# The way into head 0: a third late down chunk, half a token chunk ahead of the heads, and decay gates by token

## The chip, the cores and the metric

One NeuronCore of a Trainium2 chip runs the whole program; the other seven do nothing. The metric is the device time of one execution in microseconds (us). An execution is made of instructions on five engines that run side by side and wait for each other through semaphores: TensorE (PE, matrix products and transposes; its weight loads are shown as PEld), VectorE (DVE), ScalarE (ACT), GpSimd (POOL) and SyncE (SP, which only issues DMAs here).

## What is computed

Two transformer-like blocks over one sequence of 256 tokens with 1024 channels, all in float32. The change lies where the first feed-forward of the second block ends and its mixer begins:

```python
h = h + 0.5 * swiglu(rmsnorm(h, ffn1_norm[l]), ffn1_w_in[l], ffn1_w_out[l])
h = h + hybrid_mixer(rmsnorm(h, mix_norm[l]), w_in[l], ...)

def hybrid_mixer(u, w_in, ...):
    proj = (u @ w_in).astype(f32)
    (hq, hf, hi, hg, gq, gk, gv, ga, gb, gz, gate_h, gate_g) = jnp.split(proj, offsets, axis=-1)
    ...
    qkv = jax.nn.silu(causal_short_conv(jnp.concatenate([gq, gk, gv], axis=-1), conv_w))
    ...
    beta = jax.nn.sigmoid(gb)
    g = -jnp.exp(a_log.astype(f32)) * jax.nn.softplus(ga + dt_bias)
```

`ga` and `gb` are 16 columns each: the decay gates, 32 columns of `w_in` for all heads together. Every other part of `proj` is wide and is cut by head. `g` goes through a cumulative sum over chunks of tokens and then multiplies the scores of every head.

## The kernel before

**Numbers.** Every weight chunk (128 x 2048 values, 1 MB) comes from memory into a ring of three slots `w_raw`. ScalarE rounds it into `w_hi` (line 623, or in two halves line 630), VectorE takes the rest into `w_lo` (line 1160), and TensorE makes three products per tile: high by high, high by low, low by high, in the one-pass format fp32r. The activations are split the same way into `xa_hi` and `xa_lo`. In all, each chunk costs ScalarE one copy, VectorE one subtraction, and TensorE 48 products with 256 moving columns or 24 with 512.

**The ring sets the order.** Chunks have a global number. The copy into `w_hi` of chunk c waits until TensorE has done chunk c-3 (`gemm_done`), and the load of c waits for the `w_lo` of c-3 (`lo_ready`). Each engine's program is written out by hand in its own order, and an engine takes its instructions strictly in that order.

**The end of the feed-forward** (`ffn`, `last_rows`). Hidden tiles come two to a step: `up` chunks make them, ScalarE and VectorE turn them into `xb`, and a `down` chunk adds their part of the result into PSUM. The last step runs up, up, down, up, up, and then two down chunks together in `last_rows`: tokens 0 to 127 of both (semaphore `y_first`), then tokens 128 to 255 (`y_half`, `gemm_done`). Behind each VectorE adds the residual (line 1403), ScalarE makes the norm's factor and VectorE applies it (line 1517).

**The seam** (`normed`, `first_gemm`, lines 2090 to 2099). TensorE transposes tokens 0 to 127 (line 2083, 8 transposes), runs 2 filler products (`spin`, line 2088), transposes the other half of the tokens, and multiplies chunk `ba`, of which only 32 columns are used later, as 24 products of 256 columns with the weights stationary (lines 2017 to 2022). So the gates come out by channel; `ab_turned` (line 2410) turns them by token inside head 0.

**Head 0** (`head(0, True, False)`). A head has 6 chunks: q and k of the delta rule (chunk 0), v (1), q and f of the other mixer (2), gates (3) and two token chunks (4 and 5), which have the tokens stationary and 512 moving columns. TensorE cuts them into 24 quarters: 0 to 15 for the first four (12 products of 256 columns each), 16 to 23 for the token chunks (6 products of 512 columns each). Between the quarters lie the small products of the recurrences; head 0 has only those that prepare its own data:

- VectorE runs the short convolution as 12 taps (line 1681) when chunks 0 and 1 are out; ScalarE applies SiLU (line 1049), squares (line 1053); TensorE sums the squares and turns v behind quarter 15 (lines 2658 and 2661).
- `sums_of_g` (lines 2417 and 2418) makes the cumulative sums of the gates, and behind the squares four transposes (line 2680) spread them; VectorE makes the decay exponents from them (line 1884, `lt_pre`).
- After quarters 16 to 19 come the products of keys and queries (line 2692, waiting for `lt_pre`), then quarters 20 and 21, the transposes of the first inverse (line 2704, waiting for `y0_ready`), and quarters 22 and 23.
- VectorE closes with the last use of the exponents (line 1916, `lt2_ready`), a copy of the token results (line 1920), and half a `w_lo`.

Heads 1 to 7 run in a loop and begin with `inv_z` (line 2554, waiting for `lt2_ready`), a transpose (line 2579) and quarter 0, whose last four products use `w_lo` (line 2503, `weights_ready`).

## Time and profile before

| what | us |
|---|---|
| median of 3 runs (1386.59 to 1386.94) | 1386.69 |
| the profiled execution | 1387.09 |
| its span in the profile | 1385.3 |
| granted TensorE clock in it | 0.999 of full |
| TensorE busy | 1368.4 |
| VectorE busy | 1026.5 |
| ScalarE busy | 804.6 |

"Busy" counts the time in which an engine has at least one instruction under way. A matmul row of the timeline is longer than the distance to the next one, since matmuls are pipelined, so costs of matmuls are read from the distance of their starts. The chain of waits follows the work that ended last back to front.

### The profile page before, as it was taken

How to read it: one execution, taken by the hardware profiler on the slowest of the kernel's cores; microseconds unless marked ns; L12 is line 12 of the kernel's file. 1: busy time of each engine (PE TensorE's matmuls, PEld its weight loads, DVE VectorE, ACT ScalarE, POOL GpSimd, SP SyncE). 2: the span in 40 equal slices, each digit the busy share in tenths (PEclk: the TensorE clock that was granted, in tenths of full speed). 3: DMA queues.
4: the chain of work that ended last, by engine and by line, in shares of the span. 5: the costliest groups of instructions: out<-in, count | busy, mean ns of one | idle time of the engine just before them, and what ended most of it. 6: DMA issues, size and time to landing. Idle time of an engine off the chain costs nothing.

```text
span 1385.3 us, 25247 instructions
## 1 busy us (share of the span) xinstructions
PE 1368.4 (99%) x9092; PEld 1238.7 (89%) x9092; DVE 1026.5 (74%) x1602; ACT 804.6 (58%) x1311; POOL 23.8 (2%) x71
## 2 busy tenths in 40 slices
PE   8999999999999999999999999999999999999998
PEld 8999999988888888888899999999999898888887
DVE  5786786677666686666788888888888877666665
ACT  4444554644344354444678898898898844544444
POOL 6000000000000000000000000000000000000000
PEclk9999999999999999999999999999999999999999
DMA  8565555556555746556564544535534276566661
GB/s 264 150 191 145 146 147 161 185 184 209 185 182 189 233 132 207 182 182 192 152 174 131 132 117 135 142 102 154 134 103 147 85 190 213 153 204 195 197 193 61
DMA packets 298383, 227.82 MB, mean 164 GB/s; under 512 B 10882, under 2 KB 280404, under 8 KB 298324
## 3 DMA queue, kind: packets, MB, share of 16 engines
q1 hardware_dynamic: 298180, 226.75, 55.3%
q8 instruction: 40, 0.66, 0.2%
q10 hardware_dynamic: 144, 0.26, 0.1%
q14 instruction: 19, 0.16, 0.0%
HBM read 225.90 MB, written 1.08 MB: 164 GB/s over the span
## 4 chain that ended last, share of the span: by engine, by line
PE 94%; DVE 3%; ACT 2%; DVEq 1%; issue 1%; POOL 0%; ACTq 0%; POOLq 0%
PE G L1988 9%; PE G L1990 8%; PE G L1989 8%; PE M L2005 7%; PE G L2005 7%; PE M L1993 7%; PE M L1994 7%; PE M L1995 7%; PE G L2007 4%; PE M L2007 4%; PE G L2728 2%; PE G L2108 2%; PE G L1993 2%; PE G L1995 2%; PE G L1994 2%; PE M L2554 1%
## 5 line engine op out<-in xcount | busy, mean ns | idle before, releaser
L1160 DVE TENSOR_TENSOR w_lo<-w_raw,w_hi 128x2048 fp32r<-128x2048 f32 (+2 forms) x249 | 480.3, 1935 | 156.9 <-ACT w_hi L623 153.8
L623 ACT ACTIVATE w_hi<-w_raw 128x2048 fp32r<-128x2048 f32 x198 | 377.9, 1909 | 174.0 <-PE G L1990 75.3
L1988 PE MATMUL G<-xa,w_hi 128*128 128x256 f32 x992 | 292.2, 295 | 0.0
L1990 PE MATMUL G<-xa,w_lo 128*128 128x256 f32 x992 | 280.2, 282 | 0.0
L1989 PE MATMUL G<-xa,w_hi 128*128 128x256 f32 x992 | 280.1, 282 | 0.0
L1988 PEld LDWEIGHTS G<-xa,w_hi 128*128 128x128 f32 x992 | 189.4, 191 | 1.9 <-DVE w_lo L1160 0.7
L1989 PEld LDWEIGHTS G<-xa,w_hi 128*128 128x128 f32 x992 | 189.5, 191 | 0.0
L1990 PEld LDWEIGHTS G<-xa,w_lo 128*128 128x128 f32 x992 | 189.1, 191 | 0.0
L1993 PE MATMUL M<-w_hi,xb 128*128 128x512 f32 x304 | 118.9, 391 | 0.6 <-DVE xb L1160 0.5
L1994 PE MATMUL M<-w_lo,xb 128*128 128x512 f32 x304 | 118.7, 390 | 0.0
L1995 PE MATMUL M<-w_hi,xb 128*128 128x512 f32 x304 | 118.3, 389 | 0.0
L2005 PE MATMUL M<-xa,w_hi 128*128 128x512 f32 x408 | 102.4, 393 | 0.0
L2005 PE MATMUL G<-xa,w_hi 128*128 128x512 f32 x408 | 101.3, 390 | 0.0
L833 ACT ACTIVATE arena<-arena 128x256 f32<-128x256 f32 x38 | 15.9, 418 | 138.3 <-DVE arena L1564 138.3
L2005 PEld LDWEIGHTS G<-xa,w_hi 128*128 128x128 f32 x408 | 75.3, 188 | 14.8
L2005 PEld LDWEIGHTS M<-xa,w_hi 128*128 128x128 f32 x408 | 73.4, 189 | 13.1
L1993 PEld LDWEIGHTS M<-w_hi,xb 128*128 128x128 f32 x304 | 57.2, 188 | 12.1 <-DVE w_lo L1160 0.7
L1995 PEld LDWEIGHTS M<-w_hi,xb 128*128 128x128 f32 x304 | 57.1, 188 | 12.1
L1994 PEld LDWEIGHTS M<-w_lo,xb 128*128 128x128 f32 x304 | 57.2, 188 | 10.5
L2007 PEld LDWEIGHTS M<-xa,w_lo 128*128 128x128 f32 x408 | 55.7, 190 | 4.0
L2007 PEld LDWEIGHTS G<-xa,w_lo 128*128 128x128 f32 x408 | 55.7, 190 | 4.0
L2007 PE MATMUL G<-xa,w_lo 128*128 128x256 f32 x408 | 56.9, 282 | 0.0
(409 smaller groups left out, 2518.5 us busy)
## 6 DMA issues: line engine op xcount, KB each, us to landing
w_raw<-in_w_in SPq DMA_DIRECT2D x150, 512.0 KB, 4.8
w_raw<-in_ffn_w_in SPq DMA_DIRECT2D x88, 512.0 KB, 5.0
w_raw<-in_w_ff SPq DMA_DIRECT2D x64, 512.0 KB, 4.3
w_raw<-in_ffn_w_out SPq DMA_DIRECT2D x44, 512.0 KB, 4.8
w_raw<-in_w_in SPq DMA_DIRECT2D x33, 256.0 KB, 3.2
w_raw<-in_w_out SPq DMA_DIRECT2D x16, 512.0 KB, 4.2
w_raw<-in_w_branch_gdn SPq DMA_DIRECT2D x16, 512.0 KB, 5.3
w_raw<-in_w_branch SPq DMA_DIRECT2D x12, 512.0 KB, 4.3
```

What stands on the lines that cost most here:

```text
L623: nc.scalar.activation(w_hi[:, slot, :], w_raw[:, slot, :], ACT.Copy).then_inc(hi_ready, 1)
L1160: return v.tensor_tensor(dst, src, hi.bitcast(F32), ALU.subtract)
L1988: mm(out_, w[0], x[0], start=first, stop=False)
L1989: mm(out_, w[0], x[1], start=False, stop=False)
L1990: return mm(out_, w[1], x[0], start=False, stop=last_)
L1993: mm(out_, x[0], w[0], start=first, stop=False)
L1994: mm(out_, x[0], w[1], start=False, stop=False)
L1995: return mm(out_, x[1], w[0], start=False, stop=last_)
L2005: mm(both_parts, wh[:, k, at:at + P], xa[:, :, k, :], start=k == 0, stop=False)
L2007: ins = mm(bank[:, 0:T], wl[:, k, at:at + P], xa_hi[:, k, :], start=False, stop=k == KT - 1)
L2108: ins = mm(G[:, j, CW * i:CW * i + CW], x[:, k, P * i:P * i + P], w[j][:, k, :], start=first and k == 0, stop=last and k == KT - 1)
L2728: mm(G[:, n % 2, :].rearrange("p (h t) -> p h t", h=2), wh[:, k, :], xb[:, :, k, :], start=k == 0, stop=False)
```

## The change

- The first feed-forward's last step becomes up, up, up, up, and three down chunks in `last_rows`, in place of two. Between its last chunk's two halves and the others stand the 8 transposes of tokens 0 to 127.
- Chunk number `ba` is now head 0's first token chunk (k 0 to 3), and the first number of the heads is the decay chunk (32 columns). TensorE takes both by blocks of 128 tokens (`first_token_block`, `decay_block`), with tokens stationary; the fillers are gone, as are `first_gemm` and `ab_turned`. All other chunks of head 0 keep their slots one number later, and quarters 16 to 19 are left out of head 0.
- In head 0, `w_hi` and `w_lo` of the chunks to come are made at other places; the sum of squares stands behind quarter 12, quarter 15 behind the gates' transposes, and quarter 22 ahead of the inverse's transposes.

TensorE at the seam, before: `half_normed` and `normed1` tell that a half of tokens 128 to 255 is normed; `arena` holds them, and `M<-masks,ident` is the filler.

```order
L2083 MATMUL M<-ident,arena 128x128 x7
L2088 MATMUL M<-masks,ident 128x512 x2
L2083 MATMUL M<-ident,arena 128x128 [waits half_normed]
L2083 MATMUL M<-ident,arena 128x128 x3
L2083 MATMUL M<-ident,arena 128x128 [waits normed1]
L2083 MATMUL M<-ident,arena 128x128 x3
L2017 MATMUL G<-xa,w_lo 128x256 [waits xh_ready,evac0,lo_ready]
L2018 MATMUL G<-xa,w_hi 128x256
```

The same place now, from the last products of the first token block to the first of the decay block:

```order
L2438 MATMUL M<-w_hi,xa 128x512 [waits xl_ready]
L2438 MATMUL M<-w_hi,xa 128x512 x3
L2110 MATMUL M<-ident,arena 128x128 [waits half_normed]
L2110 MATMUL M<-ident,arena 128x128 x3
L2447 MATMUL G<-w_hi,xa 128x32 [waits lo_ready,xh_ready,evac0]
L2448 MATMUL G<-w_lo,xa 128x32
```

The filler and the 256-column products are gone; 512-column token products and 32-column decay products stand around the transposes.

VectorE in head 0, before, from the `w_lo` of head 0's fourth chunk (two halves) over the taps to the sums of the gates:

```order
L1160 TENSOR_TENSOR w_lo<-w_raw,w_hi 128x1024 [waits hi_ready] x2
L1681 SCALAR_TENSOR_TENSOR arena<-arena 128x256 [waits tap_ready]
L1681 SCALAR_TENSOR_TENSOR arena<-arena 128x256 x5
L1681 SCALAR_TENSOR_TENSOR arena<-arena 128x256 [waits tap_ready]
L1681 SCALAR_TENSOR_TENSOR arena<-arena 128x256 x5
L1827 COPY arena<-M 128x2x8x2 [waits gsum_done]
L1829 TENSOR_TENSOR arena<-arena,M 128x8x2
```

The same place now (the first row is the `w_lo` of the chunk of q and f):

```order
L1182 TENSOR_TENSOR w_lo<-w_raw,w_hi 128x1024 [waits hi_ready] x2
L1712 SCALAR_TENSOR_TENSOR arena<-arena 128x256 [waits tap_ready]
L1712 SCALAR_TENSOR_TENSOR arena<-arena 128x256 x5
L1182 TENSOR_TENSOR w_lo<-w_raw,w_hi 128x2048 [waits hi_ready]
L1712 SCALAR_TENSOR_TENSOR arena<-arena 128x256 [waits tap_ready]
L1712 SCALAR_TENSOR_TENSOR arena<-arena 128x256 x5
L1182 TENSOR_TENSOR w_lo<-w_raw,w_hi 128x2048 [waits hi_ready]
L1861 COPY arena<-M 128x2x8x2 [waits gsum_done]
```

One whole `w_lo` has moved in between the two groups of taps, and another behind them, ahead of the sums.

VectorE at the end of head 0, before, from the last use of the key products to the end of the head's code:

```order
L1703 TENSOR_TENSOR arena<-arena 128x256 x2
L1913 TENSOR_TENSOR arena<-M,arena 128x256
L1916 SCALAR_TENSOR_TENSOR arena<-M,arena 128x384 x2
L1920 COPY arena<-G 128x512 [waits tok_done]
L1160 TENSOR_TENSOR w_lo<-w_raw,w_hi 128x1024 [waits hi_ready]
```

and now:

```order
L1734 TENSOR_TENSOR arena<-arena 128x256 x2
L1950 TENSOR_TENSOR arena<-M,arena 128x256
L1953 SCALAR_TENSOR_TENSOR arena<-M,arena 128x384 x2
L1957 COPY arena<-M 128x512 [waits tok_done]
L1182 TENSOR_TENSOR w_lo<-w_raw,w_hi 128x2048 [waits hi_ready]
```

The last `w_lo`, that of head 1's first chunk, is whole here; before, its first half stood earlier, right behind the copy of line 1889.

The diff, cut to its core:

```diff
-        def ffn(c0, w_up, w_down):
+        def ffn(c0, w_up, w_down, late=False):
...
-            with sp.Fori(0, 5) as i:
+            with sp.Fori(0, 4 if late else 5) as i:
...
+            if late:
+                for n in range(4):
+                    load_two(c0 + 26 + n, (c0 + 26 + n) % RING, w_up, P * (18 + n), FF2 + P * (18 + n))
+                for n in range(2):
+                    load_rows(c0 + 30 + n, (c0 + 30 + n) % RING, w_down, 16 + 2 * n)
...
+        ffn(FIRST["ffn1"], w_up1, w_down1, True)
...
-        load_cols(c, c % RING, w_in2, O_GA)
-        c0 = FIRST["heads"]
+        load_tok(c, c % RING, 0, 0)
+        slot_free(c0)
+        for k in (0, KT // 2):
+            sp.dma_start(decay_cols(w_raw)[:, k:k + KT // 2, :], w_in2[:, k:k + KT // 2, O_GA:O_GA + 2 * VH]
+                         ).then_inc(w_loaded[c0 % RING], 16)
...
-                load_two(c0 + j + h * 6, (c0 + j) % RING, w_in2, left + h * step, right + h * step)
+                at = c0 + j + (1 if isinstance(h, int) and h == 0 else 0)
+                load_two(at + h * 6, at % RING, w_in2, left + h * step, right + h * step)
...
-            for part in range(2):
+            for part in (1,) if isinstance(h, int) and h == 0 else range(2):
                 load_tok(c0 + 4 + part + h * 6, (c0 + 4 + part) % RING, part, h)
...
-        ffn(c0, 0)
+        ffn(c0, 0, True)
         rms_first(summed0, 1)
+        split(c0 + 30 + RING)
+        x_hi_block(3, 0)
         split(c0 + 31 + RING)
         rms_half(half_summed, 1)
         rms_rest(summed1, 1)
-        x_hi(3)
+        x_hi_block(3, 1)
         split(c0 + 32 + RING)
 
         nc.scalar.activation(lb, lb, ACT.Exp)
         nc.scalar.activation(lb1, lb1, ACT.Exp).then_inc(lb_exp, 1)
         c = FIRST["ba"]
         split(c + RING)
-        act.wait_ge(decay_step, 2)
...
-                act.wait_ge(gemm_done, c0 + j + 1 + i * 6)
+                act.wait_ge(gemm_done, c0 + j + (1 if main or not gemm else 2) + i * 6)
...
             first_tap(0)
             z_copy(5)
             y_copy(4)
+            if not main:
+                split_j(1)
             raw_copy(1)
             first_tap(2)
+            if not main:
+                split_j(2)
...
-            if gemm:
+            if main and gemm:
                 split_part(c0 + 1 + RING, 0, i, 6)
...
-            split_j(2)
+            if main:
+                split_j(2)
...
+                    c = c0 + 2 + (2 if final and late else 3) * u
                     for n in range(2):
-                        hidden(c + n, i, 6, n, (1 + u) % 2 * 2 + n, h0 + 2 + 2 * u + n + i * 4,
-                               isinstance(i, int) and u == 1 and n == 1)
+                        hidden(c + n, i, 6, n, 4 + n if final and late and u == 1 else (1 + u) % 2 * 2 + n,
+                               h0 + 2 + 2 * u + n + i * 4, final and u == 1 and n == 1)
                         w_low(c + n + RING, i, 6)
-                    if not (isinstance(i, int) and u == 1):
+                    if not (final and (late or u == 1)):
                         w_low(c + 2 + RING, i, 6)
...
+        ffn(c0, H_FFN1, True)
+
+        def first_turned():
+            w_low(c0 + 30 + RING)
+            x_low_part(3, 0, 0)
+
+        def decay_low():
+            dve.wait_ge(hi_ready, c0 + 31 + RING + 1)
+            low_of(decay_cols(w_lo), decay_cols(w_raw), decay_cols(w_hi)).then_inc(lo_ready, 1)
+            x_low_part(3, 0, 1)
+
+        sum_and_norm(3, c0 + 33, 0.5, 4, gain_mix, decay_low, first_turned)
+        x_low_block(3, 1)
         w_low(c0 + 32 + RING)
-
-        dve.wait_ge(gemm_done, FIRST["ba"] + 1)
-        v.tensor_copy(ab_t, G[:, 0, 0:T]).then_inc(evac[0], 1)
-        v.drain().then_inc(decay_step, 1)
...
-        dve.wait_ge(ab_done, 1)
-        v.tensor_copy(abx, M[:, 5, 0:4 * VH].rearrange("p (i h) -> p i h", i=TT))
+        dve.wait_ge(gemm_done, FIRST["heads"] + 1)
+        v.tensor_copy(abx, G[:, 0, 0:4 * VH].rearrange("p (i h) -> p i h", i=TT)).then_inc(evac[0], 1)
...
                 w_low_half(FIRST["yh"] + 1, 1)
             tap(2, 0)
             tap(3, 0)
+            if not main:
+                w_low_j(1)
             tap(1, 2)
...
             tap(3, 2)
             if not main:
+                w_low_j(2)
                 dve.wait_ge(gsum_done, 1)
...
-                w_low_half(c0 + 1 + RING, 0, i, 6)
+                if main:
+                    w_low_half(c0 + 1 + RING, 0, i, 6)
...
-            w_low_j(2)
+            if main:
+                w_low_j(2)
...
-                w_low_half(c0 + 3 + RING, 0, i, 6)
+                if main:
+                    w_low_half(c0 + 3 + RING, 0, i, 6)
...
-                v.tensor_copy(tok[:, 0, :], G[:, 1, :]).then_inc(evac[1], 1)
-                w_low_half(c0 + 3 + RING, 1, i, 6)
+                v.tensor_copy(tok[:, 0, :], G[:, 1, :] if main else M[:, 4, :]).then_inc(evac[1], 1)
+                if main:
+                    w_low_half(c0 + 3 + RING, 1, i, 6)
+                else:
+                    w_low_j(3)
...
+            if turn:
+                turn()
             for h in range(2):
                 for k in range(2):
                     ins = row_half(slots[last], x[last], 1, k, h, False, k == 1)
@@ -2086,17 +2113,6 @@
...
-                    c = c0 + 2 + 3 * u
+                    c = c0 + 2 + (2 if final and late else 3) * u
...
-                    if not (final and u == 1):
+                    if not (final and (late or u == 1)):
                         down(c + 2, i, 6, u, u + i * 2, first and u == 0)
...
+            tiles = (0, 2, 4) if late else (2, 0)
+            first_down = 33 - len(tiles)
...
-            last_rows([(c0 + 31 + n) % RING for n in range(2)], [x_rows(xb_hi, xb_lo, r) for r in (2, 0)], down_ready)
-
-        ffn(FIRST["ffn1"], EV_FFN1, H_FFN1, 2, 3, 2, True)
...
+            last_rows([(c0 + first_down + n) % RING for n in range(len(tiles))], [x_rows(xb_hi, xb_lo, t) for t in tiles], down_ready,
+                      block_turned)
+
+        def mix_turned():
+            pe.wait_ge(normed0, 4)
+            transposed(tmp, 0, 0)
+            transposed(tmp, 0, 1)
+
+        ffn(FIRST["ffn1"], EV_FFN1, H_FFN1, 2, 3, 2, True, mix_turned)
+
+        def first_token_block(b):
+            c = FIRST["ba"]
+            wh, wl = rows4(w_hi, c % RING), rows4(w_lo, c % RING)
+            out_, blk = M[:, 4 if b == 0 else 0, :], slice(P * b, P * b + P)
+            pe.wait_ge(xh_ready, 4 * 3 + 2 * b + 1)
+            weights_ready(c)
+            for k in range(4):
+                mm(out_, xa_hi[:, k, blk], wh[:, k, :], start=k == 0, stop=False)
+                mm(out_, xa_hi[:, k, blk], wl[:, k, :], start=False, stop=False)
+            pe.wait_ge(xl_ready, 4 * 3 + 2 * b + 1)
+            for k in range(4):
+                mm(out_, xa_lo[:, k, blk], wh[:, k, :], start=False, stop=False)
+
+        def decay_block(b):
...
+            out_, blk = G[:, 0, 2 * VH * b:2 * VH * b + 2 * VH], slice(P * b, P * b + P)
+            pe.wait_ge(xh_ready, 4 * 3 + 2 * b + 2)
+            weights_ready(c)
+            for k in range(KT):
+                mm(out_, xa_hi[:, k, blk], wh[:, k, :], start=k == 0, stop=False)
+                mm(out_, xa_hi[:, k, blk], wl[:, k, :], start=False, stop=False)
+            pe.wait_ge(xl_ready, 4 * 3 + 2 * b + 2)
+            for k in range(KT):
+                ins = mm(out_, xa_lo[:, k, blk], wh[:, k, :], start=False, stop=k == KT - 1)
+            return ins
+
+        first_token_block(0)
+        pe.wait_ge(half_normed, 4)
+        transposed(tmp, 1, 0)
         pe.wait_ge(evac[0], EV_BA)
-        first_gemm(c % RING, G[:, 0, :], 3, 1)
-
-        def ab_turned():
-            pe.wait_ge(decay_step, 1)
-            for i in range(TT):
-                at = 2 * VH * i
-                ins = nc.tensor.transpose(M[:, 5, at:at + 2 * VH], ab_t[0:2 * VH, P * i:P * i + P],
-                                          ident[0:2 * VH, 0:2 * VH])
-            ins.then_inc(ab_done, 1)
+        decay_block(0)
+        pe.wait_ge(normed1, 4)
+        transposed(tmp, 1, 1)
+        first_token_block(1)
+        decay_block(1).then_inc(gemm_done, 2)
 
...
-                slot, bank = (c0 + j) % RING, (j + 1) % 2
+                at = j if main else j + 1
+                slot, bank = (c0 + at) % RING, (j + 1) % 2
...
-                if not main and l == 1:
-                    ab_turned()
...
+            def squares_summed():
+                pe.wait_ge(sq_ready, i + 1)
...
+                ins.then_inc(vt_done, 1)
+
             quarter(12)
+            if not main:
+                squares_summed()
...
-            if not main:
-                quarter(15)
-            if gemm:
...
+            if main and gemm:
+                squares_summed()
...
-            quarter(16)
-            quarter(17)
-            quarter(18)
-            quarter(19)
+                nc.tensor.transpose(M[0:3 * VH, 5, P:2 * P], gams.rearrange("p h i e -> p (h i e)"), ident[:]).then_inc(gam_done, 1)
+            if main:
+                quarter(16)
+                quarter(17)
+                quarter(18)
+                quarter(19)
+            else:
+                quarter(15)
             if gemm:
                 pe.wait_ge(qn_ready, i + 1)
+                if not main:
+                    pe.wait_ge(v_ready, i + 1)
                 pe.wait_ge(lt_pre, i + 1)
...
             quarter(20)
             quarter(21)
+            if not main:
+                quarter(22)
```

## Rows read from the trace of the kernel before

**Rows 1.** The profile page: the span, and the busy time of each engine.

```profile
span 1385.3 us, 25247 instructions
...
PE 1368.4 (99%) x9092; PEld 1238.7 (89%) x9092; DVE 1026.5 (74%) x1602; ACT 804.6 (58%) x1311; POOL 23.8 (2%) x71
```

**Rows 2.** Timeline of TensorE (start, us, engine, line, operation, shapes, idle before), 682 to 690 us.

```profile
682.46 1.03 PE L2083 MATMUL M<-ident,arena 128*128 128x128 f32 x8
...
683.33 1.88 PE L2088 MATMUL M<-masks,ident 128*128 128x512 f32 x4
...
685.58 1.32 PE L2083 MATMUL M<-ident,arena 128*128 128x128 f32 x8 [0.37 <-DVE arena L1517]
...
687.02 0.35 PE L2017 MATMUL G<-xa,w_lo 128*128 128x256 f32 x1
...
689.96 0.28 PE L2498 MATMUL G<-xa,w_hi 128*128 128x256 f32 x1
```

**Rows 3.** The chain of waits (start, us, what), 682 to 683 us.

```profile
682.16 0.23 PE M L1994
...
682.65 0.70 DVE res L1403
```

**Rows 4.** Timeline, all engines, 108.7 to 108.9 us and 704.6 to 705.3 us.

```profile
108.78 0.22 PE L2270 MATMUL M<-xb 128*128 128x128 f32 x1
...
108.83 0.39 PE L2269 MATMUL M<-xb 128*128 128x384 f32 x1
...
704.66 0.54 PEld L2417 LDWEIGHTS M<-arena,tri 128*128 128x128 f32 x4
...
705.12 0.30 PEld L2418 LDWEIGHTS M<-arena,ones 128*128 128x128 f32 x2
```

**Rows 5.** Timeline of ScalarE, 687 to 710 us.

```profile
690.22 1.92 ACT L623 ACTIVATE w_hi<-w_raw 128x2048 fp32r<-128x2048 f32 x1 [0.69 <-PE G L2022]
...
707.37 1.06 ACT L1049 ACTIVATE arena<-arena 128x1024 f32<-128x1024 f32 x1 [0.48 <-DVE arena L1681]
...
708.98 0.63 ACT L1053 ACTIVATE arena<-arena 128x512 f32<-128x512 f32 x1
```

**Rows 6.** Timeline of VectorE, 693 to 733 us.

```profile
693.73 2.28 DVE L1160 TENSOR_TENSOR w_lo<-w_raw,w_hi 128x2048 fp32r<-128x2048 f32 x1
...
695.93 0.22 DVE L1627 COPY arena<-M 128x64 f32<-128x64 f32 x1
...
699.39 2.36 DVE L1160 TENSOR_TENSOR w_lo<-w_raw,w_hi 128x1024 fp32r<-128x1024 f32 x2
...
701.67 5.66 DVE L1681 SCALAR_TENSOR_TENSOR arena<-arena 128x256 f32<-128x256 f32 x12
...
717.63 1.65 DVE L1884 TENSOR_SCALAR arena<-M,arena 128x128 f32<-128x128 f32 x6
...
727.09 0.68 DVE L1920 COPY arena<-G 128x512 f32<-128x512 f32 x1
...
727.69 1.22 DVE L1160 TENSOR_TENSOR w_lo<-w_raw,w_hi 128x1024 fp32r<-128x1024 f32 x1
...
732.00 0.76 DVE L1747 COPY_PREDICATED arena<-masks,M 128x256 f32<-128x256 int32 x1 [1.90 <-PE M L2570]
```

**Rows 7.** Timeline of TensorE, 692 to 731 us.

```profile
692.93 0.30 PE L2410 MATMUL M<-ident,arena 32*128 32x32 f32 x2
...
714.09 1.02 PE L2658 MATMUL M<-arena,ones 128*128 128x512 f32 x2
...
715.38 0.60 PE L2680 MATMUL M<-ident,arena 128*128 128x128 f32 x4
...
728.68 0.62 PE L2554 MATMUL M<-arena 128*128 128x128 f32 x4
...
729.14 0.38 PE L2579 MATMUL M<-ident,arena 128*128 128x128 f32 x2
...
730.32 0.64 PE L2503 MATMUL G<-xa,w_lo 128*128 128x256 f32 x4
```

More of the change, by code:

```diff
@@ L2008, in wide_gemm @@
             ins.then_inc(gemm_done, 1)
-        def first_gemm(slot, bank, n, groups=2):
-            wh, wl = cols(w_hi, slot), cols(w_lo, slot)
-            for j in range(groups):
-                out_, at = bank[:, T * j:T * j + T], slice(P * j, P * j + P)
-                for k in range(KT):
-                    if j == 0 and k % 4 == 0:
-                        pe.wait_ge(xh_ready, 4 * n + 3 + k // 4)
-                    mm(out_, wl[:, k, at], xa_hi[:, k, :], start=k == 0, stop=False)
-                    mm(out_, wh[:, k, at], xa_hi[:, k, :], start=False, stop=False)
-                for k in range(KT):
-                    if j == 0 and k % 4 == 0:
-                        pe.wait_ge(xl_ready, 4 * n + 2 + k // 2)
-                    ins = mm(out_, wh[:, k, at], xa_lo[:, k, :], start=False, stop=k == KT - 1)
-            ins.then_inc(gemm_done, 1)
         def col_gemm(slot, bank, widths=(P, P), between=None):
@@ L2057, in row_gemm, with last_rows @@
             ins.then_inc(gemm_done, 1)
-        def last_rows(slots, x, ready):
+        def last_rows(slots, x, ready, turn=None):
             last = len(slots) - 1
@@ L2353, in _, with ffn @@
         last_rows([(c0 + 29 + n) % RING for n in range(3)], [x_rows(xb_hi, xb_lo, 2 * ((13 + n) % 3)) for n in range(3)], ff_ready)
-        def ffn(c0, ev, h0, n_x, n_norm, spins, second_late):
+        def ffn(c0, ev, h0, n_x, n_norm, spins, second_late, block_turned=None):
+            late = block_turned is not None
             def turn(n):
@@ L2376, in steps @@
                 for u in range(2):
-                    c = c0 + 2 + 3 * u
+                    c = c0 + 2 + (2 if final and late else 3) * u
                     for n in range(2):
@@ L2380, in steps @@
                            (lambda: turn(1)) if first and u == 0 and n == 0 else None)
-                    if not (final and u == 1):
+                    if not (final and (late or u == 1)):
                         down(c + 2, i, 6, u, u + i * 2, first and u == 0)
@@ new lines, in decay_block @@
+        def decay_block(b):
+            c = FIRST["heads"]
+            wh, wl = decay_cols(w_hi), decay_cols(w_lo)
+            out_, blk = G[:, 0, 2 * VH * b:2 * VH * b + 2 * VH], slice(P * b, P * b + P)
[8 more added lines that the diff above has]
+            return ins
@@ L2653, in head @@
                 hgrn_turned()
[L2654 to L2663 removed]
+            if main and gemm:
+                squares_summed()
             if main:
```

88 lines of the change are left out of this document (38 added, 50 removed).

## The prediction

> **What bounds the kernel now.** I read the page first: TensorE is busy for 1368.4 of a span of 1385.3 us [rows 1], so only what it waits for, or work taken from it, can be won, and any new wait is paid in full. Next the timeline of TensorE over the seam. The last down product leads straight into the transposes at 682.46, and quarter 0 of head 0 starts at 689.96 [rows 2]: 7.50 us. In them lie 16 transposes and the 24 products of the gates. The products run from 687.02 to 689.96, 2.94 us or about 0.12 each; a transpose costs 0.11 (8 of them from 682.46 to 683.33) [rows 2], so 16 cost 1.76. The rest, 7.50 - 2.94 - 1.76 = 2.8 us, is dead: the filler of line 2088 and waits for the norm. That is all the seam can give back. VectorE takes the last residual at 682.65 [rows 3], and the transposes of the second half start at 685.58 [rows 2]: the norm's hand-over is 3.1 us from the last product.
>
> Then head 0. From its quarter 0 at 689.96 [rows 2] to the first products with `w_lo` in head 1 at 730.32 [rows 7] it takes 40.36 us. The reader is to see that TensorE hardly waits there, and how VectorE and ScalarE hand work back and forth [rows 5, 6].
>
> **The seam, part by part.** Times for the changed kernel continue the clock of the trace.
>
> The feed-forward's end has the same products in another order. With three down chunks the first half of the tokens is complete one chunk and a half ahead of the end, so the norm of tokens 0 to 127 is hidden. The eight transposes stand before the last 12 products of 512 columns. The `w_lo` of the last down chunk comes about when its first block wants it; I add 0.2. So the last down product ends at 682.46 + 0.9 + 0.2 = 683.55.
>
> Token block 0: 12 products of 512 columns at 0.23 [rows 3] = 2.75, until 686.3. The second half is normed 3.1 after the last product, at 686.65: a wait of 0.35. Four transposes 0.45: 687.1. Decay block 0: 24 products. Four transposes 0.45, token block 1 2.75, decay block 1 24 products. `xa_hi` and `xa_lo` of each half are ready in time, since a token block or a decay block stands between their transposes and them.
>
> The price of a product with 32 moving columns isn't in the trace for fp32r. Nearest rows: 4 weight loads for products of 16 columns took from 704.66 to 705.12, 0.115 each [rows 4]. The other end: a 128-column fp32r product whose weights were already in place gave way to the next after 0.05 (108.78 to 108.83) [rows 4]. Each of the 48 needs a load of 128 columns, since each product in the trace has its own, so I take 0.11: 48 x 0.11 = 5.3; the low end is 48 x 0.05 = 2.4. The Trainium skill (TensorE: Matmul & The Clock Gate, "LDWEIGHTS (loading the stationary operand)") gives a load the number of columns divided by 1.2 in ns, 107 ns for 128. The trace's 0.115 agrees.
>
> Sum: 683.55 + 2.75 + 0.35 + 0.45 + 2.65 + 0.45 + 2.75 + 2.65 = 695.6 for quarter 0, against 689.96: +5.6. The tokens' products brought forward are worth 4 quarters of 6 x 0.23 = 5.5. So the seam by itself wins nothing (+0.1): the 2.8 dead us are eaten by the decay products, 5.3 in place of 2.94, and the waits of 0.35 and 0.2.
>
> **Head 0.** It loses 5.5 us of quarters 16 to 19, and the turning of the gates (two transposes, 0.30 with their tail, 0.45 with the restart behind them [rows 7]). With no new wait it would take 40.36 - 5.95 = 34.4 us. But VectorE and ScalarE have a chain of their own, which the removed quarters covered. Counted from quarter 0's start:
>
> - `w_hi` of the chunk of v can't start before the decay products end, since both numbers are reported there: 0.26 after (in the trace 689.96 to 690.22, 1.92 long [rows 2, 5]): 2.2. Its `w_lo`: start to the copy of the gates 2.2 (693.73 to 695.93): 4.4. From that copy to the start of the next `w_lo` 3.46 (695.93 to 699.39), from there to the taps 2.28 (to 701.67) [rows 6]: 10.1.
> - Six taps are half of 5.66 [rows 6]: 12.95. The new `w_lo` between them costs 2.2: 15.2. Six more taps: 18.0.
> - SiLU to the end of the squares takes 2.2 (707.37 to 708.98 + 0.63) [rows 5]: 20.3. TensorE is through 13 quarters of 12 x 0.12 = 1.44 and the sums of the gates (6 loads at 0.115, 0.7) at 19.4. It waits **0.95**.
> - Sum of squares and turning v 1.3 (714.09 to 715.38 [rows 7]), quarters 13 and 14 2.9, the gates' transposes 0.45 and a hand-over of 0.2: 25.15 is where line 1884 starts. It takes 1.65 [rows 6], to 26.8; TensorE has turned the gates and done quarter 15 at 26.5, so the key products wait **0.35**.
> - From line 1884 everything runs on VectorE: its start to the copy of the token results took 9.46 (717.63 to 727.09), to the `w_lo` behind it 10.06 (727.69) [rows 6]. A whole `w_lo` is 2.28. So `w_lo` of head 1's first chunk is ready at 25.15 + 10.06 + 2.28 = 37.5. Nothing in that stretch waited for the first half of the `w_lo` that stood there, so moving it out wins nothing and adds 1.1 at the end. TensorE wants lines 2503's operand 1.64 after it enters head 1 (728.68 to 730.32 [rows 7]); `lt2_ready` lets it enter at 25.15 + 9.46 = 34.6, so it arrives at 36.3 and waits **1.2** for this `w_lo`.
>
> So 37.5 us in place of 40.36: -2.85. Against the 34.4 without waits that is 3.1: the 0.95 + 0.35 + 1.2 above, and the 0.6 that is left falls to `y0_ready` and `lt2_ready`. What is queued behind the late `w_lo` on VectorE are head 1's first level products and the inverse of line 1747; VectorE idled 1.90 before that one [rows 6], so its backlog of 1.3 relative to TensorE is taken up there.
>
> The loads are not late: SP's slots come free 5 us or more before ScalarE wants the data. Only head 1's gates chunk and the decay rows queued behind it go out later with the last `w_lo`, and they are wanted some 10 us after.
>
> **Sum.** +5.6 - 2.85 = +2.8 us. It is made against the profiled execution (1387.09 with a span of 1385.3); the median of the three runs is 1386.69, 0.4 less, and the difference is applied there: **1389.5**. The bounds: the decay products down to 2.4 us (-2.9); the new waits anywhere from none (-3.1) to all of them with VectorE's backlog paid again in head 1 (+1.9).
>
> **Rivals.**
>
> *The small products go at the pace of their columns.* 48 x 0.05 = 2.4 in place of 5.3. For it: the pair at 108.78. Against: that pair had a longer product before it that hid the load, and here no product is long enough. Total 2.8 - 2.9: 1386.6, not slower. The Trainium skill (same page, "Back-to-back issue gap") has about 60 cycles for products of up to 64 columns; by that figure 48 of them are an estimated 1.2 us, and the sum would be 1385.4. The 16-column rows speak against it.
>
> *The chain in head 0 is shorter than TensorE's own work.* The place is the `w_lo` between the taps and the one at the head's end. It decides from where conv, squares and exponents are ready by 19.4 and 26.5 after quarter 0, and the last `w_lo` by 36.3. For it: each of my terms is a start-to-start distance that may hold idle time. Against: the taps and `w_lo`s of rows 6 are back to back. None of the 3.1 us: 1386.4, not slower.
>
> *The backlog is paid again.* ScalarE ends head 0 about 0.7 late and VectorE 1.3; if both are on TensorE's path in head 1, 1.9 more: 1391.4. For it: the inverse and the levels go to and fro in every quarter. Against: the idle 1.90 before line 1747.
>
> **How the numbers follow.** The forecast has 0.52, its own range 1388.3 to 1390.6. The small products at column pace 0.12, the chain hidden 0.20, the backlog paid again 0.16. The range takes in all down to 1386.4 and up to 1391.3, with a tail left out on either side. About 0.2%, 2.8 us, is what a measurement of this kernel can tell from no change; the forecast lies on that edge. Slower by more: a little over half of the forecast and the backlog, 0.44. Faster by more needs the first two rivals together, 0.04. Within: 0.52.
>
> **What would show it.** In the changed kernel's profile: 24 rows of the decay block 2.6 us long; quarter 0 about 5.6 us later; TensorE waiting about 1 us before the sum of squares, for ScalarE's squares; about 1.2 us before the first products with `w_lo` of head 1, for VectorE's line 1182; head 1 to 8 as long as before. The forecast is wrong if the decay block takes 1.2 us, or if TensorE has no idle row between quarter 12 and head 1.

## The result, and the profile after

| | median us | runs | against before |
|---|---|---|---|
| before | 1386.72 | 6, 1386.59 to 1386.94 | |
| changed | 1393.99 | 6, 1392.70 to 1395.91 | 1.0052 [1.0039, 1.0065] |
| forecast | 1389.5 | range 1386.4 to 1391.3 | |

The changed kernel is 7.3 us slower, and its runs lie 3.2 us apart where those of before lie 0.35 apart. The sign of the forecast (+2.8) was right, its size was not, and the time is outside the range. The mean granted clock of TensorE belongs to the result: 0.999 in the two runs at 1392.7, 0.998 in those at 1393.9 and 1394.0, 0.997 at 1394.4 and 0.996 at 1395.9. The last is the profiled one. One run of the last version below (1909.8 us at a mean granted clock of 0.655) was disturbed and is left out of everything that follows.

First the page of the changed kernel, against [rows 1].

```profile
span 1394.2 us, 25250 instructions
PE 1373.7 (99%) x9110; PEld 1243.3 (89%) x9110; DVE 1024.3 (73%) x1598; ACT 803.3 (58%) x1310; POOL 23.3 (2%) x71
```

The span grew by 8.9 us and TensorE's busy time by 5.3, with only 18 more instructions in the records. So more than half of the loss does not show as idle time. Next the timeline of TensorE over the seam, the answer to [rows 2].

```profile
681.08 1.03 PE L2110 MATMUL M<-ident,arena 128*128 128x128 f32 x8
...
684.70 0.39 PE L2434 MATMUL M<-w_hi,xa 128*128 128x512 f32 x1
684.92 0.39 PE L2435 MATMUL M<-w_lo,xa 128*128 128x512 f32 x1
...
687.82 0.66 PE L2110 MATMUL M<-ident,arena 128*128 128x128 f32 x4 [0.24 <-DVE arena L1542]
688.23 0.26 PE L2447 MATMUL G<-w_hi,xa 128*128 128x32 f32 x1
688.34 0.26 PE L2448 MATMUL G<-w_lo,xa 128*128 128x32 f32 x1
...
690.02 1.48 PE L2451 MATMUL G<-w_hi,xa 128*128 128x32 f32 x8
691.34 1.11 PE L2110 MATMUL M<-ident,arena 128*128 128x128 f32 x4
692.10 0.78 PE L2434 MATMUL M<-w_hi,xa 128*128 128x512 f32 x1
692.68 0.63 PE L2435 MATMUL M<-w_lo,xa 128*128 128x512 f32 x1
693.10 0.63 PE L2434 MATMUL M<-w_hi,xa 128*128 128x512 f32 x1
...
699.93 0.36 PE L2550 MATMUL G<-xa,w_hi 128*128 128x256 f32 x1
```

Three things are to be seen. The price of the decay products was right: 688.23 to 688.34 is 0.11. The token block starts at 684.70 instead of 683.55, so something ahead of it is late. And from 690.02 the same instructions take longer: 8 decay products take 1.32 instead of 0.9, four transposes 0.76 instead of 0.45. Quarter 0 comes at 699.93; the forecast had 695.6.

The windows say why. The columns are the stretch, its length, the busy time and count of TensorE's products, TensorE's weight loads, VectorE, ScalarE and GpSimd, then TensorE's granted clock, the DMA share and GB/s.

```profile
688.00:690.00 2.00, 2.00 (x20) 2.00 (x20) 1.12 (x2) 0.60 (x1) 0.00 (x0) 1.00 1.20 290
690.00:691.00 1.00, 1.00 (x9) 1.00 (x8) 0.00 (x0) 0.00 (x0) 0.00 (x0) 0.73 1.20 291
691.00:697.00 6.00, 6.00 (x19) 4.94 (x19) 2.77 (x2) 2.59 (x4) 0.00 (x0) 0.50 0.16 39
697.00:698.00 1.00, 1.00 (x9) 0.94 (x7) 0.78 (x5) 0.00 (x0) 0.00 (x0) 0.86 0.00 0
698.00:700.00 2.00, 2.00 (x20) 2.00 (x19) 0.25 (x2) 0.00 (x0) 0.00 (x0) 1.00 0.80 179
700.00:701.00 1.00, 1.00 (x9) 1.00 (x9) 0.00 (x0) 0.82 (x1) 0.00 (x0) 0.85 1.12 337
701.00:704.00 3.00, 3.00 (x16) 3.00 (x16) 1.88 (x1) 1.09 (x1) 0.00 (x0) 0.50 0.46 118
705.00:709.00 4.00, 4.00 (x36) 4.00 (x35) 2.65 (x10) 3.78 (x9) 0.00 (x0) 1.00 0.82 233
```

The clock falls to 0.50, 1.2 GHz in place of 2.4, twice, each time in or just behind a decay block, and TensorE's row shows it busy throughout. A 512-column product there follows the last after 0.42 or 0.43 us (692.68 to 693.10) instead of 0.23. In before the clock is 1.00 over the same place, idle time and all.

Then the waits of TensorE from the last down products on. The columns are what TensorE had to do, whom it waited for, the sum, the times and the longest.

```profile
PE M L2033 <- DVE w_lo L1182: 1.6, 1, 1.6
PE M L2606 <- DVE arena L1778: 1.2, 3, 0.5
PE G L2555 <- DVE w_lo L1182: 0.8, 1, 0.8
...
PE M L2606 <- DVE arena L1953: 0.3, 1, 0.3
PE M L2750 <- DVE arena L1920: 0.3, 1, 0.3
```

The first is the lateness ahead of the token block. It is in a down product, at a place where I had looked only for 0.2. The rows around it, VectorE's and then TensorE's:

```profile
661.43 0.68 DVE L1589 TENSOR_REDUCE arena<-G 128x256 f32<-128x512 f32 x1
665.51 2.29 DVE L1182 TENSOR_TENSOR w_lo<-w_raw,w_hi 128x2048 fp32r<-128x2048 f32 x1 [1.38 <-ACT w_hi L637]
667.72 0.41 DVE L1584 TENSOR_TENSOR arena<-arena,G 128x256 f32<-128x256 f32 x1
668.62 0.42 DVE L1182 TENSOR_TENSOR xb<-arena,xb 128x256 fp32r<-128x256 f32 x1 [0.48 <-ACT xb L849]
670.43 2.29 DVE L1182 TENSOR_TENSOR w_lo<-w_raw,w_hi 128x2048 fp32r<-128x2048 f32 x1 [1.38 <-ACT w_hi L637]
```

```profile
670.80 0.39 PE L2035 MATMUL M<-w_hi,xb 128*128 128x512 f32 x1
672.77 0.50 PE L2033 MATMUL M<-w_hi,xb 128*128 128x512 f32 x1 [1.59 <-DVE w_lo L1182]
673.11 0.39 PE L2034 MATMUL M<-w_lo,xb 128*128 128x512 f32 x1
```

From 670.80 to 672.77 is 1.97 where 0.23 is normal, and the next product is 0.11 late as well: 1.86 us lost. ScalarE makes the chunk's `w_hi` only behind its copy of the last hidden tile (`xb`), and VectorE waits 1.38 us for it.

In head 0 the waits after 699.93 were the forecast's own. TensorE's rows:

```profile
720.86 1.02 PE L2672 MATMUL M<-arena,ones 128*128 128x512 f32 x2
727.46 0.67 PE L2750 MATMUL M<-arena 128*128 128x256 f32 x2 [0.29 <-DVE arena L1920]
735.29 0.70 PE L2606 MATMUL M<-arena 128*128 128x128 f32 x4 [0.33 <-DVE arena L1953]
738.00 0.74 PE L2555 MATMUL G<-xa,w_lo 128*128 128x256 f32 x4 [0.84 <-DVE w_lo L1182]
```

The squares show no wait, because TensorE itself was late by the second dip. The last `w_lo` was complete 38.0 us after quarter 0; the forecast had 37.5.

### The profile page after: what moved, and what is told of

Its sections match the earlier page's. It is cut to its first block, busy times and chain, and to the rows that moved or that the text cites. A ratio compares the mean times of both kernels' runs of the same rounds, so it can differ in the third digit from the quotient of the medians.

```text
span 1394.2 us, 25250 instructions
## 1 busy us (share of the span) xinstructions
PE 1373.7 (99%) x9110; PEld 1243.3 (89%) x9110; DVE 1024.3 (73%) x1598; ACT 803.3 (58%) x1310; POOL 23.3 (2%) x71
## 4 chain that ended last, share of the span: by engine, by line
PE 90%; DVE 4%; ACT 3%; DVEq 1%; issue 1%; POOL 0%; ACTq 0%; POOLq 0%
PE G L2028 8%; PE G L2030 8%; PE G L2029 8%; PE M L2045 6%; PE G L2045 6%; PE M L2033 6%; PE M L2034 6%; PE M L2035 6%; PE M L2047 3%; PE G L2047 3%; PE G L2789 2%; PE G L2124 2%; PE G L2033 2%; PE G L2035 2%; PE G L2034 2%; PE M L2606 1%
```

## The experiments

My theory after this: the forecast's terms stand, and what it lacks is (a) a low granted clock brought on by the products with 32 moving columns and (b) the late `w_lo` of the last down chunk. The rivals were that the clock falls through the waits of the new seam, or that the extra time is VectorE's and ScalarE's in head 0. Every run below is compared with the kernel before, timed beside it at 1386.8 to 1386.9.

### 1. The decay products with more columns (wide, wide128)

```diff
-            wh, wl = decay_cols(w_hi), decay_cols(w_lo)
-            out_, blk = G[:, 0, 2 * VH * b:2 * VH * b + 2 * VH], slice(P * b, P * b + P)
+            wh, wl = cols(w_hi, c % RING), cols(w_lo, c % RING)
+            out_, blk = G[:, 0, CW * b:CW * b + CW], slice(P * b, P * b + P)
```

With 128 columns the slices are `[:, :, 0:P]` of the same. In both, VectorE's copy of the gates picks out the 32 columns that count.

> The changed kernel, with 256 moving columns in each of the 48 decay products instead of 32 (the other 224 are computed and not used). Theory: the products with 32 moving columns bring TensorE's granted clock to 0.50. In the profile of the changed kernel it stood there for about 6 us in the seam and 3 us in head 0, which cost 3.3 + 0.6 us, and again differently in each run. With 256 columns a product takes 0.12 instead of 0.11, 48 x 0.01 = 0.5 us more, but the clock stays at 1.00 from the down products to head 1: about 1394.0 - 3.9 + 0.5 = 1390.6, quarter 0 of head 0 at about 697.2 instead of 699.93. Rival (the clock falls through the waits and the transposes of the seam, not through the narrow products): the dip stays, 1394 to 1395. Second rival (the extra time is waits for VectorE and ScalarE in head 0): no less than 1394.

> The changed kernel with 128 moving columns in each of the 48 decay products instead of 32 (96 of them computed and not used). By its weight load a product costs the same as with 32, 0.11 us; with 256 columns it was 0.12. Theory (few moving columns per product bring the granted clock down): with four times as many columns it stays at 1.00 as with 256, and the time is that of 256 columns less 48 x 0.01: 1392.5, with runs within 0.5 us of each other. Rival (128 columns are still too few): a dip in some runs, 1393 to 1396.

Measured: 1392.94 (1392.66 to 1393.05) and 1392.56 (1392.27 to 1392.82). The windows with 128 columns:

```profile
690.00:691.00 1.00, 1.00 (x12) 1.00 (x10) 0.10 (x1) 0.00 (x0) 0.00 (x0) 1.00 1.19 290
691.00:697.00 6.00, 6.00 (x44) 5.52 (x44) 3.27 (x4) 2.59 (x4) 0.00 (x0) 1.00 0.19 46
```

There are 44 products in the six microseconds that held 19. The clock stays up and the spread is gone: 0.5 us instead of 3.2. Against the profiled execution of the changed kernel quarter 0 comes 2.9 us sooner:

```profile
697.03 0.34 PE L2550 MATMUL G<-xa,w_hi 128*128 128x256 f32 x1
```

The size for 256 columns was wrong, 1392.9 instead of 1390.6. I had taken the clock's cost from the worst of six runs (3.9) and set it against their median. Between the medians it is 1394.0 - 1392.6 = 1.4 us, and in the profiled run 3.5. So 3.1 us of the changed kernel's 7.3 are neither in the forecast nor in the clock.

### 2. Narrow products put into the kernel before (narrow, narrow256)

```diff
+        for n in range(48):
+            ins = mm(M[:, 4, 0:32], xa_hi[:, n % KT, P * (n % 2):P * (n % 2) + P], cols(w_hi, c % RING)[:, n % KT, 0:32],
+                     start=n == 0, stop=n == 47)
```

The second kernel has `T`, 256, in place of 32. In both, the report that the gates' products are done (`gemm_done`) stands behind the 48.

> The kernel before, with 48 more products of 32 moving columns and a weight block of 128 columns each, in one row behind the gates' products and ahead of quarter 0 of head 0; their result is not used. They stand for the decay products alone, without any other part of the change. By the price of the prediction they cost 48 x 0.11 = 5.3 us: 1392.0. Theory: the granted clock falls to 0.50 within or behind them and stays there for some microseconds, so it costs 2 to 4 us more: 1394 to 1396. Rival (the clock falls for another reason, in the changed seam or through the change in head 0): 1392.0 and a granted clock of 1.00 throughout. Second rival (their columns set the pace): 48 x 0.05 = 2.4, 1389.1.

> The kernel before with 48 added products in the same place as in the run with 32 columns, of the same weight blocks, but with 256 moving columns; their result is not used. Theory (products with few moving columns cost the clock): 48 x 0.12 = 5.8 us, granted clock 1.00 throughout, 1386.9 + 5.8 = 1392.7, with runs within 0.5 us of each other: 2.3 us less than with 32 columns, though each product has eight times the columns. Rival (48 further products in a row, or the later quarter 0, bring the clock down by themselves): a dip here too, 1395 to 1397.

Measured: 1394.99 (1393.65 to 1397.18) with 32 columns and 1392.81 (1392.69 to 1393.00) with 256. First the timeline and windows with 32, then with 256.

```profile
689.27 6.09 PE L2405 MATMUL M<-w_hi,xa 128*128 128x32 f32 x48
695.20 0.56 PE L2501 MATMUL G<-xa,w_hi 128*128 128x256 f32 x1
```

```profile
692.00:694.00 2.00, 2.00 (x20) 2.00 (x19) 0.00 (x0) 0.00 (x0) 0.00 (x0) 0.96 1.16 329
694.00:697.00 3.00, 3.00 (x15) 3.00 (x15) 1.17 (x5) 1.54 (x1) 0.00 (x0) 0.50 1.17 310
697.00:700.00 3.00, 3.00 (x16) 3.00 (x15) 2.45 (x2) 0.37 (x1) 0.00 (x0) 0.50 0.21 67
701.00:704.00 3.00, 3.00 (x26) 3.00 (x27) 1.63 (x10) 0.91 (x5) 0.00 (x0) 1.00 1.00 290
```

```profile
694.00:697.00 3.00, 3.00 (x28) 3.00 (x27) 0.85 (x4) 1.09 (x1) 0.00 (x0) 1.00 1.18 299
697.00:700.00 3.00, 3.00 (x26) 2.83 (x25) 2.62 (x4) 0.82 (x1) 0.00 (x0) 1.00 0.45 139
```

This settles the cause of the low clock. The seam and head 0 are those of before, and the 48 products have no wait among them: with 32 columns the clock falls to 0.50 and comes back some 7 us later, with 256 it stays at 1.00. With eight times the columns the kernel is 2.2 us faster. The narrow ones cost 8.1 in the median. At 0.11 each, 5.3 of it is their price, and the 2.8 that are left are the clock's.

### 3. Narrow products in turn with wide ones (turns)

```diff
+                mm(t_out, x[:, k, blk], wt[:, k, :], start=n == 0, stop=False)
+                for m in (2 * n, 2 * n + 1):
+                    x, wt, k = dec[m]
+                    ins = mm(d_out, x[:, k, blk], wt[:, k, :], start=m == 0, stop=m == 3 * KT - 1)
```

> The changed kernel, with the same 24 token products of 512 columns and 48 decay products of 32 columns, but in turn: after each token product two decay products, in both token blocks (the transposes of tokens 128 to 255 within block 0). Nothing is computed otherwise. Theory (a row of narrow products one behind another brings the granted clock to 0.50): no such row is left, and the clock stays at 1.00 at the same count of instructions: about 1394.0 - 3.9 = 1390. The VectorE wait in the seam may grow by 0.3. Rival (the narrow products cost the clock wherever they stand): the granted clock falls here too, 1393 to 1396. Rival (idle time at the seam costs the clock): same, 1393 to 1396.

Measured: 1393.60. Four runs lie from 1393.19 to 1393.76 at a mean clock of 0.999 to 1.0, and two at 1401.83 and 1401.86 with 0.992. The profiled one is of the four and has 1.00 in all windows from 683 to 710 us; it pays 1.2 us for a wait that the turns bring:

```profile
686.75 0.47 PE L2469 MATMUL M<-w_hi,xa 128*128 128x512 f32 x1 [1.21 <-DVE w_lo L1182]
```

So the first theory, that only an unbroken row of narrow products costs the clock, is not borne out. Mixed, they spare it in most runs, but the two others lost 8 us and more clock than any run of the changed kernel. They have no trace, so where they lost it stays open. With more columns the clock stayed up in every run; with the one other order that was tried it did not.

### 4. The gates by channel (chan)

The 48 products become 24 with 32 columns of weights and 256 moving columns, as in the kernel before, and the two transposes of the gates stand in head 0 again:

```diff
+                mm(out_, wl[:, k, :], xa_hi[:, k, :], start=k == 0, stop=False)
+                mm(out_, wh[:, k, :], xa_hi[:, k, :], start=False, stop=False)
...
+                if not main and l == 1:
+                    ab_turned()
```

> The changed kernel with the gates by channel, as they were before: 24 products with 32 columns of weights and 256 moving columns instead of 48 products with 32 moving columns, and the two transposes of the gates back in head 0. The three late down chunks, the half token chunk in the seam and the order of head 0 stay. Theory: it gives back 48 x 0.11 - 2.94 = 2.4 us of products and the 3.9 us of half clock, and pays 0.45 for the turning: 1394.0 - 2.4 - 3.9 + 0.4 = 1388.1; no dip of the granted clock. Rival (waits for VectorE and ScalarE are the cause): the gates are only ready later here, so the chain in head 0 gets longer: 1393 or more.

Measured: 1390.12 (1389.85 to 1390.21), clock 1.00. Here too I had subtracted the profiled run's clock from the median. From the kernel with 256 columns it is 1392.94 - 2.9 (48 x 0.12 less 24 x 0.12) + 0.4 = 1390.4, 0.3 from the run. That sum was made after the result. The trace also shows a gain behind head 0 that the sum leaves out; it is told with heads 1 to 8 below.

### 5. Three late down chunks alone (late)

```diff
-        ffn(FIRST["ffn1"], w_up1, w_down1)
+        ffn(FIRST["ffn1"], w_up1, w_down1, True)
...
+            tiles = (0, 2, 4) if late else (2, 0)
```

> The kernel before with one edit of the change alone: three down chunks instead of two stand at the end of the first feed-forward; all else as before. Theory: VectorE gets to the last chunk but two late, since the w_lo of that chunk waits behind the last hidden products (in the changed kernel TensorE waits 1.6 us for line 1182 there, of which 1.15 reach the end of the down products): 1386.9 + 1.15 = 1388.0, and the profile shows a wait of 1 to 1.6 us for a w_lo about 15 us before the seam. Rival (the wait in the changed kernel comes from its other edits at the seam): 1386.9. The prediction had 0.2 for it: 1387.1.

Measured: 1388.94 (1388.73 to 1389.34), ratio 1.0014 [1.0004, 1.0024]: +2.0, with the same wait as in the changed kernel.

```profile
PE M L2000 <- DVE w_lo L1166: 1.6, 1, 1.6
```

This part of the change, whose only price in the forecast was 0.2, costs 2.0 by itself. The 1.15 that I expected came from comparing absolute times of two executions. In the trace of the kernel with narrow products, which is the same as before up to the seam, the run of eight products with `w_lo` near 628 us starts 0.67 us earlier than in before, so such a comparison is no better than that. The gap between two neighbouring products inside one trace gave 1.86.

### 6. The late chunks and the order of head 0, one at a time (chan_half, chan_half_taps, chan_two)

These start from the gates by channel, where the clock is steady and 0.3 us can be told. The first takes back the halves of the last `w_lo` of head 0, the second also the taps' order:

```diff
-                if main:
-                    w_low_half(c0 + 3 + RING, 0, i, 6)
+                w_low_half(c0 + 3 + RING, 0, i, 6)
...
-                else:
-                    w_low_j(3)
```

```diff
-            if not main:
-                w_low_j(1)
...
-                w_low_j(2)
+                w_low_j(1)
...
+                w_low_j(2)
```

The third has two late down chunks again.

> The changed kernel with the gates by channel, and the last w_lo of head 0 in halves at the places of before, the first of them inside the order of that head. By the prediction this w_lo, moved out to the end, costs 1.1 us and is what TensorE waits for in head 1 (0.8 us in the run with the gates by channel, at the first products with w_lo). Theory: that wait goes and nothing takes its place: 1390.1 - 0.8 = 1389.3, and if VectorE's lateness is also what lengthened heads 1 to 7 by 0.5 us, 1388.8. Rival (VectorE is as late either way, the wait moves to another line): 1390.1.

> As the run before it (gates by channel, last w_lo of head 0 in halves), and the w_lo that the change puts between the taps stands behind both groups of taps, the next behind the sums: the order of head 0 as it was. Theory: the waits before the squares (0.5 us) and before line 1920's operand (0.3) go, and TensorE then waits for nothing in head 0: 0.8 less than the run without this, 1388.0 to 1388.5. Rival (the order of taps and w_lo has no part in the waits; the sums, the exponents or the w_lo moved behind them are as late): no difference, and a new wait for a w_lo in the quarters of head 0.

> The run with the gates by channel (1390.1), with two late down chunks instead of three. Theory: the 1.86 us at the w_lo of the last down chunk go; the first half of the tokens is complete 12 products later (2.75 us), and since the transposes of that half had 1.0 us to spare, they wait 1.75: 1390.0. So the third late chunk wins as much as it loses. Rival (the late chunk's wait is hidden by nothing and the norm of the first half is ready in time anyway): 1388.3. Second rival (the transposes wait for the whole 2.75 and the seam moves with them): 1391.0.

Measured: 1389.35, 1389.34 and 1390.25. The halves give the 0.8 back and no wait takes its place. Heads 1 to 7 take no less for it: from head 1 to head 7 it is 306.0 us, and 306.1 without the halves. So the further step to 1388.8, which was held possible, is out. The taps' order gives nothing: the wait before the squares goes, and one as long comes in front of a product whose `w_lo` now stands behind the taps.

```profile
714.35 0.39 PE L2028 MATMUL G<-xa,w_hi 128*128 128x256 f32 x1 [0.47 <-DVE w_lo L1183]
```

Two late chunks in place of three give back 1.86 and lose it again, since the first half's transposes now wait for its norm. That is the forecast of this run to 0.25 us, and the wait for the `w_lo` is gone from the trace. In its place stands:

```profile
PE M L2113 <- DVE arena L1542: 2.0, 2, 1.7
```

### 7. The `w_lo` of the last down chunk sooner (chan_half_early)

```diff
+                if last and late:
+                    split(c + RING, i, step)
                 act.wait_ge(ffn_step, 2 * k + 2)
...
+                if last and late:
+                    w_low(c + RING, i, step)
                 dve.wait_ge(hh_ready, k + 1)
```

> As the run with the gates by channel and the last w_lo of head 0 in halves (1389.35), and at the end of the first feed-forward ScalarE and VectorE make w_hi and w_lo of the last down chunk before the two numbers of the last hidden tile, instead of behind them. Theory: in the run with three late down chunks alone TensorE lost 1.86 us at this w_lo (1.75 before the product and 0.11 behind it), and that was nearly all it lost. VectorE can then have it 2.3 us earlier, and the hidden tile's numbers 2.2 later, about when the third of the late chunks wants them: 1.4 to 1.9 us less, 1387.5 to 1387.9. Rival (the wait moves to the hidden tile, h_ready, at the same place): 1389.3 to 1390. Either way not below the kernel before.

Measured: 1387.37 (1387.10 to 1387.69), ratio 1.0003 [0.9993, 1.0012]: 1.98 less, a little more than the 1.4 to 1.9 expected. The wait is gone, and nothing came in its place. VectorE's rows:

```profile
667.89 0.41 DVE L1588 TENSOR_TENSOR arena<-arena,G 128x256 f32<-128x256 f32 x1
668.44 2.29 DVE L1186 TENSOR_TENSOR w_lo<-w_raw,w_hi 128x2048 fp32r<-128x2048 f32 x1
670.65 0.42 DVE L1186 TENSOR_TENSOR xb<-arena,xb 128x256 fp32r<-128x256 f32 x1
```

### 8. The best version (chan_half_early_split)

```diff
             if not main:
-                w_low_j(1)
+                w_low_half(c0 + 1 + RING, 0, i, 6)
             tap(1, 2)
...
+                w_low_half(c0 + 1 + RING, 1, i, 6)
                 w_low_j(2)
```

> The best of the versions so far (gates by channel, last w_lo of head 0 in halves, w_lo of the last down chunk early; 1387.37), and the w_lo that stands between the taps in head 0 in two halves, the first between the taps, the second behind them. Theory: with the whole of it between the taps the squares came 0.5 us late, with the whole behind them a product wanted it 0.5 us too early; with a half on each side SiLU and squares come 1.1 us sooner and the w_lo is complete 2.2 us later than now, 1.7 before its product. Both waits go: 0.5 us less, 1386.9, which is the time of the kernel before, not below it. Rival (TensorE arrives at the next hand-over, line 1931 in head 0 or the inverse behind it, 0.5 us earlier and waits there instead): 1387.4.

Measured: 1387.00 beside 1386.83 for before, ratio 1.0002 [0.9993, 1.0010]. The 0.4 us are at the edge of what can be told. The wait before the squares is gone from the trace; of the other, 0.2 is left. This version cannot be told from the kernel before and does not beat it.

## Why the prediction was wrong, by its own steps

The way from forecast to result is: 1389.5, + 1.7 for the late `w_lo` (1.86 in place of 0.2), + 1.3 for heads 1 to 7 and the rest behind them, = 1392.5, where the kernel with 128-column decay products has 1392.56; + 1.4 for the clock = 1394.0. The 1.7 and 1.3 are read from traces, the 1.4 is a difference of medians, so the fit is good to some tenths only. Neither of the two signs that were to show the forecast wrong came: the decay block takes 2.6 and TensorE does idle in head 0. Both looked past the places where it failed.

- **"48 x 0.11 = 5.3".** As a price it was right to the digit (688.23 to 688.34). The step failed because it was taken for the whole cost. The product's rate was weighed between 0.05 and 0.11, and the clock of everything around it was taken to stay at 1.00. Runs 1 and 2 show that it does not: 0 to 3.5 us by run, 1.4 in the median. The range had no case for it.
- **"The `w_lo` of the last down chunk comes about when its first block wants it; I add 0.2."** This step failed too, and it is the largest single miss that a run isolates: 1.86 in place of 0.2. The late chunk lets TensorE run through products ahead of ScalarE and VectorE, whose order at the feed-forward's end I didn't follow row by row as I did in head 0. Run 5 shows the loss alone, run 7 shows it undone.
- **"Quarter 0 at 695.6".** With the clock up it came at 697.03, which is 1.43 more. Counted inside each trace, from the run of eight products with `w_lo` near 628 us that both kernels share, quarter 0 comes 61.15 us later in before and 68.52 with 128 columns. That is 7.37 more where the forecast had 5.6, so the miss is 1.8, and the `w_lo` accounts for 1.7 of it. The wait for the norm, forecast at 0.35, was 0.24.
- **"37.5 us in place of 40.36" in head 0.** The mechanism was right, and so was the sum. With 128 columns it is 37.4 from quarter 0 to the first products with `w_lo` of head 1 (697.03 to 734.42). The waits came where the forecast put them: 0.5 or 0.6 idle before the squares in every kernel of the new order of the taps whose clock stayed up, 0.3 at line 1920, 0.3 at line 1953, and 0.84 at the last `w_lo`, where 0.95, 0.35, 0.6 and 1.2 were forecast. A row shows less idle time than the wait costs. From the starts of the products in the trace with 128 columns the four products that waited start 0.7, 0.45, 0.5 and 1.0 late, 2.7 in all against the forecast's 3.1. That the whole comes out to 0.1 is therefore in part luck: TensorE's own work took about 0.3 more than the 34.4 of the sum.
- **"Heads 1 to 8 as long as before".** Not quite. From head 1 to head 7 before takes 305.6 us, the kernel with 128 columns 306.4, and what follows is another 0.5 longer. With the gates by channel and the whole `w_lo` still at the end of head 0 it is 306.1 and 0.1, and the halves change nothing in that. So 0.7 of the 1.3 comes with the gates by token and not with VectorE's late `w_lo`. More than half of it is one wait 60 us behind the start of head 7, which all four kernels with gates by token have and none with gates by channel:

```profile
1100.64 0.71 PE L2606 MATMUL M<-arena 128*128 128x128 f32 x4 [0.45 <-DVE arena L1778]
```

Why the layout of the gates reaches so far stays open, and so do the 0.6 that are left. The third rival wanted 1.9 more in head 1; head 1 took 0.3 more with 128 columns (51.24 in place of 50.90) and 0.17 more with the gates by channel.
- **The rivals.** The decay block at the pace of its columns is out. The chain hidden in head 0 is out: TensorE does wait. The hoped-for gain of the seam, that 2.8 dead us are filled, was real but small: the dead time went, and the decay products took it all, as the forecast said.

The best version shows the balance of the idea itself. Rid of the narrow products and both late `w_lo`s it is level with before. Read inside the traces of the two kernels, the way from the products near 628 us to quarter 0 takes 3.7 more for 5.5 of products brought forward, so the seam wins 1.8. Head 0 takes 4.0 less where 5.5 went out, so it gives back 1.5, since its quarters were the cover of VectorE's and ScalarE's chain. Heads 1 to 7 and what follows them take 0.6 more, for a reason that no run shows.

## What to carry to other kernels

Count the products with few moving columns as two costs, their own and the clock of what follows, and read the granted clock of the stretch before you read waits; here two more transposes turned 48 products into 24 with 256 moving columns, which took 2.4 us less than 48 with 128 columns (1392.56 to 1390.12) and kept the clock up. When work is put behind a row of products so that TensorE runs longer without a break, look at who makes the operands of the last of them. Work that is brought forward to fill a hole is taken from somewhere, so ask first what it was hiding there.

## What the runs showed of the hardware

- The granted clock fell to 0.50 with TensorE shown busy for every microsecond of the stretch, within or behind 24 to 48 products with 32 moving columns. With 128 or 256 columns in the same places it stayed at 1.00. It also stayed there through the 1.6 us in one piece in which TensorE waited for the last down chunk. In the kernel where each two narrow products followed one of 512 columns it stayed at 1.00 in the profiled run, and two of six runs had a mean clock of 0.992. At 0.50 a 512-column product took 0.43 us. The Trainium skill (TensorE: Matmul & The Clock Gate, "Wait — 56ns, not 53.3ns?") has 426.7 ns for it at 1.2 GHz, and the trace agrees. The same page, "What's actually happening", ties the lower clock to how busy the engine has recently been; here its busy row was full and the clock fell all the same, so the busy row of a profile does not tell it.
- The cost differs from run to run of one kernel: 1392.7 to 1395.9 and 1393.7 to 1397.2 with narrow products in a row, 1393.2 to 1401.9 with narrow ones in turn with wide ones, but at most 1 us apart in every kernel without them.
- A product of 32 columns and one of 128 columns, each with its load of 128 columns of weights, cost the same 0.11 us (688.46 to 688.57 in the changed kernel, 688.75 to 688.86 with 128 columns), and one of 256 columns 0.12. Narrowing it below 128 columns won nothing here.
